# Decay rows spread by one transfer a head, rope tables by one transfer, and the last mLSTM head's statistics behind the first attention masks

## The chip, the cores and the metric

The kernel runs on one core of one Trainium2 chip. The metric is the device time of one execution in microseconds, as the median of several runs. TensorE (PE) multiplies, VectorE (DVE), ScalarE (ACT) and GpSimd (POOL) do the elementwise work, and transfers (DMA) are issued from the queues of SyncE (SP), ScalarE and GpSimd; all of them share the core's 16 DMA engines. Matrices go through TensorE as pairs of a rounded high part and a low part, three products for one.

## The reference

One block of a hybrid model, 512 tokens of width 1024, in float32. Half of the width is attention with 8 heads of 64, half is an mLSTM with 4 heads of 128.

```python
h = rms_norm(x, pre_norm_g)
proj = h @ w_in                      # 1024 -> 4*512 + 5*512 + 4 + 4
aq, ak, av, az, mq, mk, mv, mo, mz, mi, mf = split_columns(proj)

# attention: rotary positions on the first 16 of 64 dimensions of each head, causal softmax
ya = moba_attention(partial_rope(aq, pos), partial_rope(ak, pos), av)
ya = rms_norm(ya, attn_out_g) * silu(az)

# mLSTM: causal convolution over 4 tokens, gates mi, mf, decays between tokens
qk = silu(causal_depthwise_conv(concat([mq, mk]), conv_w, conv_b))
hm = mlstm_chunkwise(q, k * 128 ** -0.5, mv, mi + i_bias, mf + f_bias)
#   s = (q . k) * exp(D - m_t), D a causal matrix from sums of log-gates
#   h = num / max(|nq|, exp(-m_t))
hm = (hm - mean) * rsqrt(var + 1e-6) * mlstm_out_g
ym = sigmoid(mo) * hm * silu(mz)

y = concat([ya, ym]) @ w_out
out = x + rms_norm(y, post_norm_g)
```

## The kernel before, in words

The token axis is cut into 4 tiles of 128. The projection runs through 74 weight slots of 512 columns (SLOTS), the output through 16 more; a slot's weights come by one load of SyncE (L564) into one of 4 raw buffers, are rounded by ScalarE to a high part (L783, `cut`), and VectorE, or GpSimd for the last ones, takes the low part (L1070, L673, L677), after which the raw buffer is free for the load four slots on. All engines run programs written out by hand; each has a loop over the slot number b in which the work that goes beside that slot stands in a fixed order, with semaphores between engines. TensorE works slot b while ScalarE and VectorE cut slot b + 6. So each engine's queue is strictly in order: what waits holds what stands behind it.

The mLSTM is computed in its full 512 by 512 form, head by head. For head h and key tile j TensorE makes scores in bank 6 (`head_scores`), VectorE multiplies them by decays (`weighted`, L1198), ScalarE and VectorE split the result, and TensorE multiplies by the values (`head_values`). The next scores wait for `weighted`, since they use the same bank. The decays are exp(g[key] terms + g[query] terms): a row of 512 query terms for each of the 4 heads, kept in `rows[4]` (16 rows: 4 copies of 4 heads), must be spread over all 128 partitions. GpSimd makes the rows (L651) and writes them to memory (L653, `g_dram`). ScalarE's queue issues four transfers a head (`decay_rows`, L851), each of which reads one row, or its last 384, 256 or 128 elements, 128 times: the part of the row that key tile j needs. GpSimd adds the causal mask to the first 128 columns of each part (`decay_mask`, L659), waiting for all four, and ScalarE takes the exponential (`decays`, L841). All of this is for one head at a time in one buffer, so the rows of head h + 1 go out when the last tile of head h is weighted. For head 0 they go out at slot 16, and its exponentials stand at slots 20 and 21.

The rotary tables: ScalarE scales them by the norm of each token (L859), TensorE transposes them, ScalarE copies them out (L864), GpSimd writes them to memory (four times 16 KB, L683) and spreads them over the 8 heads by two transfers, one for cosines and one for sines (L687). VectorE uses them in `kq_rows` (L1263 and on).

`head_stats` (L1218 to L1239) takes mean and variance of two token tiles of an mLSTM head and `head_norm` (L1241 to L1249) normalises them; between the two stands a reciprocal root on GpSimd (`head_rsqrt`, L644). There are 8 of each. The last, number 7, is taken at the last slot (b = 64) by VectorE, and its norm at step 1 of the attention.

The attention is a second loop, over steps s, 32 units of a tile and a head (`unit`). In step s VectorE masks the scores (`mask`, L1383), ScalarE takes the exponential (L988), TensorE transposes, and the rest of the projection (the gates mz and mo), the turns and the output products are spread over the steps by a table (EVENTS). Around its start VectorE also takes the low parts of the queries (`q_low`, L1281), and gates (`mz_gate`, L1342); GpSimd multiplies the mLSTM rows by their gains (`ym_gain`, L712) and by the gate (`ym_gate`, L718), and VectorE finishes them (`z_gate`, L1350).

## Time and profile before

| | before |
|---|---|
| median of 3 runs | 320.37 us (319.39 to 320.59) |
| the profiled execution, its own time | 319.19 us |
| span of that execution, first to last instruction | 317.4 us |
| TensorE matmul busy | 307.7 us (97%) |
| VectorE busy | 223.6 us (70%) |
| ScalarE busy | 165.1 us (52%) |
| GpSimd busy | 88.1 us (28%) |
| granted TensorE clock, mean | 0.991 |
| moved by DMA | 38.30 MB, mean 121 GB/s |

Times of instructions count from the start of the span. Busy time of TensorE is the time in which a matmul is in flight, so a busy TensorE may still be fed below its best pace; consecutive starts show the pace. The granted clock is 1.0 at the full 2.4 GHz and 0.5 at 1.2 GHz. The chain that ended last is followed backwards from the end of the program, at each step to what released it. A wait for several semaphores is put down to the one that came last.

### The profile page before, as it was taken

The numbers are of one execution on the slowest core, as the hardware profiler recorded it, in microseconds if no ns is written. First come the engines' busy times: TensorE is split into PE (matmuls) and PEld (weight loads), VectorE is DVE, ScalarE is ACT, GpSimd is POOL, SyncE is SP. The second block draws the span as 40 slices with busy tenths as digits, with TensorE's granted clock in tenths as the row PEclk, the third lists the DMA queues.
The fourth block names the chain that finished last, engine by engine and source line by source line (L and its number), as shares of the span: only waits on it lengthen the run. The fifth ranks groups of instructions, "written<-read, shape, count | busy, mean of one in ns | idle before, by whom it ended". The sixth has DMA issues, their size and how long they took to land.

```text
span 317.4 us, 5020 instructions
## 1 busy us (share of the span) xinstructions
PE 307.7 (97%) x1607; PEld 258.1 (81%) x1607; DVE 223.6 (70%) x510; ACT 165.1 (52%) x339; POOL 88.1 (28%) x104
## 2 busy tenths in 40 slices
PE   8999999997999999999999999999999999999992
PEld 5788888876888888888888889978888888888882
DVE  2544899915999579976999547995577766856534
ACT  3467684548337421594243763485556976453201
POOL 4501003043541004000040006596711984000000
PEclk9999999997999999999999999999999999999998
DMA  7933463666452556753456423312220374310111
GB/s 219 322 77 91 127 191 86 140 158 183 112 111 68 160 101 177 230 166 93 124 172 208 134 74 94 102 33 69 66 66 2 126 187 153 135 66 1 68 66 66
DMA packets 30601, 38.30 MB, mean 121 GB/s; under 512 B 2664, under 2 KB 17872, under 8 KB 30576
## 3 DMA queue, kind: packets, MB, share of 16 engines
q1 hardware_dynamic: 27440, 34.51, 36.2%
q10 hardware_dynamic: 2464, 2.76, 5.0%
q0 software_dynamic: 672, 0.72, 0.8%
q8 instruction: 13, 0.21, 0.3%
q14 instruction: 12, 0.10, 0.1%
HBM read 33.68 MB, written 4.29 MB: 120 GB/s over the span
## 4 chain that ended last, share of the span: by engine, by line
PE 77%; DVE 11%; issue 5%; ACT 2%; DMA 2%; POOL 0%; DVEq 0%; POOLq 0%; ACTq 0%
PE bank L1512 20%; PE bank L1514 19%; PE bank L1513 19%; PE bank L1565 4%; PE bank L1869 3%; PE bank L1834 3%; PE bank L1813 3%; DMA w_raw<-in_w_in 2%; DVE w_lo L1070 2%; PE bank L1660 2%; DVE farena L1178 1%; PE bank L1763 1%; DVE rarena L1281 1%; PE bank L1545 1%; PE bank L1527 1%
## 5 line engine op out<-in xcount | busy, mean ns | idle before, releaser
L783 ACT ACTIVATE w_hi<-w_raw 128x512 fp32r<-128x512 f32 (+1 forms) x73 | 44.5, 616 | 71.2 <-PE bank L1514 47.2
L1512 PE MATMUL bank<-w_hi,xT_hi 128*128 128x512 f32 (+2 forms) x180 | 71.0, 395 | 0.4 <-DVE gy L1342 0.4
L1514 PE MATMUL bank<-w_hi,xT_lo 128*128 128x512 f32 (+2 forms) x180 | 68.0, 378 | 0.0
L1513 PE MATMUL bank<-w_lo,xT_hi 128*128 128x512 f32 (+2 forms) x180 | 67.7, 376 | 0.0
L1070 DVE TENSOR_TENSOR w_lo<-w_raw,w_hi 128x512 fp32r<-128x512 f32 (+1 forms) x66 | 45.7, 703 | 14.2 <-ACT w_hi L783 14.0
L1512 PE MATMUL bank<-xT_hi,w_hi 128*128 128x512 f32 x136 | 54.5, 401 | 0.0
L1514 PE MATMUL bank<-xT_hi,w_lo 128*128 128x512 f32 x136 | 53.5, 393 | 0.0
L1513 PE MATMUL bank<-xT_lo,w_hi 128*128 128x512 f32 x136 | 53.4, 393 | 0.0
L1514 PEld LDWEIGHTS bank<-w_hi,xT_lo 128*128 128x128 f32 x180 | 33.8, 188 | 5.8
L1512 PEld LDWEIGHTS bank<-w_hi,xT_hi 128*128 128x128 f32 x180 | 33.9, 188 | 5.5 <-issue 0.6
L1513 PEld LDWEIGHTS bank<-w_lo,xT_hi 128*128 128x128 f32 x180 | 34.0, 189 | 4.5
L1514 PEld LDWEIGHTS bank<-xT_hi,w_lo 128*128 128x128 f32 x136 | 25.8, 189 | 5.7
L1513 PEld LDWEIGHTS bank<-xT_lo,w_hi 128*128 128x128 f32 x136 | 25.9, 190 | 4.7
L1512 PEld LDWEIGHTS bank<-xT_hi,w_hi 128*128 128x128 f32 x136 | 25.8, 190 | 4.7
L644 POOL TENSOR_TENSOR vr<-vs,mhalf 128x2 f32<-128x2 f32 x8 | 5.6, 706 | 77.8 <-DVE vs L1237 77.8
L996 ACT ACTIVATE rarena<-bank 128x512 fp32r<-128x512 f32 (+3 forms) x32 | 14.0, 436 | 21.6 <-PE bank L1869 21.6
L1383 DVE CUSTOM_DVE_ANT_0 farena<-bank,causal 128x512 f32<-128x512 f32 (+3 forms) x32 | 15.3, 482 | 11.2 <-PE bank L1813 11.2
L1389 DVE TENSOR_TENSOR rarena<-bank,rarena 128x512 fp32r<-128x512 f32 (+3 forms) x32 | 15.6, 487 | 7.9 <-ACT rarena L996 7.8
L1198 DVE SCALAR_TENSOR_TENSOR farena<-bank,farena 128x512 f32<-128x512 f32 (+3 forms) x16 | 7.9, 491 | 17.1 <-PE bank L1514 17.0
L988 ACT ACTIVATE farena<-farena,mx 128x512 f32<-128x512 f32 (+3 forms) x32 | 17.9, 558 | 3.1 <-DVE mx L1383 2.9
L1178 DVE SCALAR_TENSOR_TENSOR farena<-farena,pcol 128x512 f32<-128x512 f32 x24 | 18.8, 783 | 0.9
L1869 PE MATMUL bank<-ident,farena 128*128 128x128 f32 x80 | 14.7, 281 | 0.0
(212 smaller groups left out, 563.8 us busy)
## 6 DMA issues: line engine op xcount, KB each, us to landing
w_raw<-in_w_in SPq DMA_DIRECT2D x66, 256.0 KB, 2.9
w_raw<-in_w_out SPq DMA_DIRECT2D x16, 256.0 KB, 2.6
kq_rows<-stage SPq DMA_DIRECT2D x8, 256.0 KB
gy<-kq_rows SPq DMA_DIRECT2D x8, 256.0 KB, 3.5
gy<-in_x SPq DMA_DIRECT2D x4, 512.0 KB, 5.3
out_y<-gy SPq DMA_DIRECT2D x7, 256.0 KB, 2.1
w_raw<-in_w_in SPq DMA_DIRECT2D x8, 196.0 KB, 3.5
farena<-in_x SPq DMA_DIRECT2D x4, 256.0 KB, 4.7
```

Source lines behind the costliest of these rows:

```text
L783: a.activation(hi, raw, ACT.Copy).then_inc(w_hi_done, 1)
L988: a.activation(prob[:, s % 2, 0:n], sm[:, s % 2, 0:n], ACT.Exp, scale=-1.0, bias=mx[:, s:s + 1], accum_out=rsum[:, s:s + 1]).then_inc(prob ...
L996: a.activation(pT[:, 2 * (u % 2), 0:n], bank[4 + u % 2][:, 0:n], ACT.Copy).then_inc(pt_hi, 1)
L1070: v.tensor_tensor(lo, raw, hi, ALU.subtract).then_inc(w_lo_done[n % 2], 1)
L1178: ins = v.scalar_tensor_tensor(out=acc, in0=u[:, j:j + SEQ], scalar=tap[j], in1=acc, op0=ALU.mult, op1=ALU.add)
L1383: v.tensor_tensor_reduce(sm[:, s % 2, 0:n], bank[6 + s % 2][:, at:at + n], causal[:, SEQ - n:], -Q_SCALE, BIG, ALU.add, ALU.min, mx[:, s:s ...
L1389: v.tensor_tensor(pT[:, 2 * (u % 2) + 1, 0:n], bank[4 + u % 2][:, 0:n], f32(pT[:, 2 * (u % 2), 0:n]), ALU.subtract).then_inc(pt_lo, 1)
L1512: pe.matmul(o, hi, m_hi, start=start, stop=False)
L1513: pe.matmul(o, hi, m_lo, start=False, stop=False)
L1514: return pe.matmul(o, lo, m_hi, start=False, stop=stop)
L1565: mm = pe.matmul(bank[t][:], xs[:, k, t * P:(t + 1) * P], ws, start=k + term == 0, stop=False)
L1869: mm = pe.transpose(bank[4 + u % 2][:, j * P:(j + 1) * P], prob[:, u % 2, j * P:(j + 1) * P], ident[:])
```

## The change

The decay parts become slices of one buffer of 1280 elements. GpSimd writes the rows of `g_dram` as 4 rows (one a head) of 1280 elements, in four transfers, one for each key tile, waits for them, and issues one transfer of 128 rows of 5 KB for a head; ScalarE issues none. For heads 1 to 3 that issue stands ahead of the reciprocal root of the head before. The rotary tables are scaled into another place in mixed order (cosine and sine of one dimension side by side), so that each row in memory holds both, and one transfer of 4 KB rows spreads them. The last head's statistics (`head_stats(7)`) go from slot 64 to step 1, behind the masks of steps 0 and 1 and the low parts of the queries; its reciprocal root on GpSimd goes to step 1; its norm goes to step 2, behind the gates; and GpSimd's four gain products go from steps 0 and 1 to steps 2 and 3.

```diff
--- before.py
+++ after.py
@@ -102,6 +102,7 @@
 R_MV, R_QK, R_P, R_KT, R_V, R_SIZE = 0, 4160, 6208, 8768, 12864, 16960
 R_PT, R_OUT, R_QT = 0, 2048, 4608
 P_AT = [0, 512, 896, 1152]
+P_END = 1280
 
 NU = NT * AH
 
@@ -313,7 +314,8 @@
                 else v.rearrange("p (a b c) -> p a b c", a=shape[0], b=shape[1])
 
         x_sb = f_part(F_X, NT, D)
-        decay = [f_part(F_E + P_AT[j], SEQ - P * j) for j in range(NT)]
+        decay_all = f_part(F_E, P_END)
+        decay = [decay_all[:, P_AT[j]:P_AT[j] + SEQ - P * j] for j in range(NT)]
         upad = f_part(F_U, 2, 516)
         cacc = f_part(F_ACC, 2, SEQ)
         pm = f_part(F_PM, 2, SEQ)
@@ -331,6 +333,7 @@
         by_dims, whole = stage, gate
         rope_t = [f_part(F_COS, SEQ), f_part(F_SIN, SEQ)]
         rope_flat = f_part(F_SIN, P)
+        rope_mixed = silu_az[:, 0, 0:P]
 
         def by_block_order(ap):
             return ap.rearrange("p (m h j) -> p h m j", m=4, h=AH)
@@ -374,8 +377,8 @@
             return blocks(w_hi[:, at]), blocks(w_lo[:, at])
 
         kq_dram = nc.dram_tensor("kq_rows", (2, AH, DH, SEQ), F32, kind="Internal").ap()
-        rope_dram = nc.dram_tensor("rope_rows", (2, ROT, SEQ), F32, kind="Internal").ap()
-        g_dram = nc.dram_tensor("g_rows", (16, SEQ), F32, kind="Internal").ap()
+        rope_dram = nc.dram_tensor("rope_rows", (ROT, 2 * SEQ), F32, kind="Internal").ap()
+        g_dram = nc.dram_tensor("g_rows", (MH, P_END), F32, kind="Internal").ap()
 
 
         x_in = [sem(f"x_in{c}") for c in range(len(X_CHUNKS))]
@@ -650,10 +653,19 @@
             g.wait_ge(gmax_done, 1)
             g.tensor_tensor(rows[4], rows[1], rows[2], ALU.subtract).then_inc(grows_done, 1)
             g.wait_ge(grows_done, 1)
-            g.dma_start(g_dram, rows[4]).then_inc(g_out, 16)
+            for j in range(NT):
+                g.dma_start(g_dram[:, P_AT[j]:P_AT[j] + SEQ - P * j], rows[4][MH * j:MH * (j + 1), j * P:])\
+                    .then_inc(g_out, 16)
+            g.wait_ge(g_out, 16 * NT)
+
+            def decay_rows(h):
+
+                if h:
+                    g.wait_ge(pm_done, NT * h)
+                g.dma_start(decay_all, g_dram[h:h + 1].to_broadcast([P, P_END])).then_inc(g_back, 16)
 
             def decay_mask(h):
-                g.wait_ge(g_back, 16 * NT * (h + 1))
+                g.wait_ge(g_back, 16 * (h + 1))
                 for j in range(NT):
                     v = decay[j][:, 0:P]
                     g.tensor_tensor(v, v, causalT[:], ALU.add).then_inc(g_masked, 1)
@@ -677,19 +689,21 @@
                     g.tensor_tensor(lo, blocks(w_raw[:, n % RAW, :]), hi.bitcast(F32),
                                     ALU.subtract).then_inc(w_lo_done[n % 2], 1)
 
+            decay_rows(0)
             decay_mask(0)
             g.wait_ge(rope_flat_done, 1)
             for t in range(NT):
-                g.dma_start(rope_dram.rearrange("q j s -> (q j) s")[:, t * P:(t + 1) * P],
+                g.dma_start(rope_dram.rearrange("j (q s) -> (j q) s", q=2)[:, t * P:(t + 1) * P],
                             rope_flat[t * 2 * ROT:(t + 1) * 2 * ROT, :]).then_inc(rope_out, 16)
             g.wait_ge(rope_out, 16 * NT)
-            for q in range(2):
-                g.dma_start(rope_t[q], rope_dram[q:q + 1].to_broadcast([AH, ROT, SEQ])).then_inc(rope_spread, 16)
+            g.dma_start(f_part(F_COS, 2 * SEQ), rope_dram.unsqueeze(0).to_broadcast([AH, ROT, 2 * SEQ]))\
+                .then_inc(rope_spread, 16)
             for t in range(NT):
                 g.wait_ge(az_done, t + 1)
                 g.wait_ge(gain_in, 16)
                 g.tensor_tensor(silu_az[:, t, :], silu_az[:, t, :], gains[:], ALU.mult).then_inc(az_gained, 1)
             for h in range(1, MH):
+                decay_rows(h)
                 head_rsqrt(2 * h - 2)
                 decay_mask(h)
                 head_rsqrt(2 * h - 1)
@@ -702,8 +716,6 @@
                 cut(b + AHEAD)
                 if b == S_MZ + 3:
                     head_rsqrt(2 * MH - 2)
-                if b == LAST_SLOT:
-                    head_rsqrt(2 * MH - 1)
 
             def ym_gain(t):
 
@@ -738,9 +750,11 @@
                     elif kind == "y_fin":
                         g.wait_ge(msy_done, i + 1)
                         rsqrt(ry[:, i:i + 1], msy[:, i:i + 1]).then_inc(ry_done, 1)
-                if s < 2:
-                    ym_gain(2 * s)
-                    ym_gain(2 * s + 1)
+                if s == 1:
+                    head_rsqrt(2 * MH - 1)
+                if 2 <= s < 4:
+                    ym_gain(2 * s - 4)
+                    ym_gain(2 * s - 3)
                 if 3 <= s < 3 + NT:
                     ym_gate(s - 3)
 
@@ -841,22 +855,14 @@
                 a.activation(decay[j], decay[j], ACT.Exp, bias=aT[:, j, 4 * j + h:4 * j + h + 1])\
                     .then_inc(decay_done, 1)
 
-            def decay_rows(h):
-
-                if h:
-                    a.wait_ge(pm_done, NT * h)
-                else:
-                    a.wait_ge(g_out, 16)
-                for j in range(NT):
-                    a.dma_start(decay[j], g_dram[4 * j + h:4 * j + h + 1, j * P:].to_broadcast([P, SEQ - j * P]))\
-                        .then_inc(g_back, 16)
-
             def rope_scale():
 
                 a.wait_ge(rope_in, 16)
                 a.wait_ge(rx_done, 1)
                 for t in range(NT):
-                    a.activation(rope_sb[:, t, :], rope_sb[:, t, :], ACT.Copy, scale=rx[:, t:t + 1]).then_inc(rope_scaled, 1)
+                    a.activation(rope_mixed[:, t * 2 * ROT:(t + 1) * 2 * ROT].rearrange("p (j q) -> p q j", q=2),
+                                 rope_sb[:, t, :].rearrange("p (q j) -> p q j", q=2), ACT.Copy,
+                                 scale=rx[:, t:t + 1]).then_inc(rope_scaled, 1)
 
             def rope_evac():
 
@@ -925,8 +931,6 @@
                     a.wait_ge(gmax_done, 1)
                     a.wait_ge(gate_clear, 1)
                     a.activation(gate_rows[32:48, :], rows[2], ACT.Copy, scale=-1.0).then_inc(gneg_done, 1)
-                if b == S_QK + 6:
-                    decay_rows(0)
                 if b == ST_AT[0]:
                     a.wait_ge(aT_done, 1)
                     a.activation(emt[:], bank[7][:].rearrange("p (t c) -> p t c", t=NT)[:, :, 32:32 + MH],
@@ -934,8 +938,6 @@
                 for h in range(MH):
                     if b - 2 in PE_ST and PE_ST[b - 2][0] == h:
                         pm_high(*PE_ST[b - 2])
-                        if PE_ST[b - 2][1] == NT - 1 and h < MH - 1:
-                            decay_rows(h + 1)
                     for c in range(2):
                         if b == S_Q[h] + 2 * c + 5:
                             conv_silu(2 * h + c)
@@ -1251,7 +1253,7 @@
             def kq_rows(w, m):
 
                 projected(v, ("ak", "aq")[w], m)
-                v.wait_ge(rope_spread, 32)
+                v.wait_ge(rope_spread, 16)
                 if w and m == 0:
                     v.wait_ge(kq_out[0], 16 * NT)
                 if m:
@@ -1320,7 +1322,7 @@
                             v_low(m)
                 if S_AQ + 6 <= b < S_AQ + 6 + NT:
                     k_low(b - S_AQ - 6)
-                if b - 2 in PE_PV and PE_PV[b - 2][1] % 2 == 1:
+                if b - 2 in PE_PV and PE_PV[b - 2][1] % 2 == 1 and b < LAST_SLOT - 1:
                     head_stats(2 * PE_PV[b - 2][0] + PE_PV[b - 2][1] // 2)
                 for h in range(MH):
                     for c in range(2):
@@ -1468,9 +1470,9 @@
                 if s < NU:
                     mask(s)
                 if s == 1:
-                    head_norm(2 * MH - 1)
                     q_low(2)
                     q_low(3)
+                    head_stats(2 * MH - 1)
                 if 0 <= s - LAG_FOLD < N_WIDE and s % 2 == 1:
                     y2_sum(s - LAG_FOLD)
                 for kind, what in events:
@@ -1486,6 +1488,8 @@
                 for kind, what in events:
                     if kind == "mz_late":
                         mz_gate(*what)
+                if s == 2:
+                    head_norm(2 * MH - 1)
                 for kind, what in events:
                     if kind == "ya_half":
                         ya_half(*what, 0)
@@ -1619,7 +1623,7 @@
 
                 pe.wait_ge(par_done, 2)
                 pe.wait_ge(rope_scaled, NT)
-                pe.transpose(bank[6][:, 0:P], rope_sb[:].rearrange("p t c -> p (t c)"), ident[:]).then_inc(rope_ps, 1)
+                pe.transpose(bank[6][:, 0:P], rope_mixed, ident[:]).then_inc(rope_ps, 1)
 
             def gate_cols():
```

## Rows read from the trace of the kernel before

**Rows 1.** Waits of TensorE in the whole span: engine, line, releaser, us, times, longest.

```profile
PE bank L1512 <- DVE farena L1198: 2.5, 1, 2.5
...
PE bank L1512 <- DVE gy L1342: 0.4, 1, 0.4
```

**Rows 2.** Busy time by stretch; then granted clock, DMA share, GB/s.

```profile
63.00:65.00 2.00, 2.00 (x10) 1.67 (x9) 0.85 (x2) 0.63 (x1) 0.00 (x0) 1.00 0.69 44
...
72.00:80.00 8.00, 6.55 (x25) 5.59 (x26) 4.91 (x9) 6.82 (x12) 3.25 (x4) 0.79 0.63 168
...
77.00:203.00 126.00, 126.00 (x624) 107.97 (x622) 101.03 (x241) 61.41 (x105) 27.52 (x30) 1.00 0.50 136
```

**Rows 3.** Chain that ended last, 61 to 73 us: start, us, what.

```profile
61.25 6.94 DMA w_raw<-in_w_in
...
70.25 1.22 ACT farena L841 x2
...
72.62 0.69 DVE farena L1198
```

**Rows 4.** Timeline of TensorE, 70 to 77 us: start, us, line, operands.

```profile
70.29 0.39 PE L1513 MATMUL bank<-w_lo,xT_hi 128*128 128x512 f32 x1
70.52 0.39 PE L1514 MATMUL bank<-w_hi,xT_lo 128*128 128x512 f32 x1
73.45 0.66 PE L1512 MATMUL bank<-rarena 128*128 128x384 f32 x1 [2.54 <-DVE farena L1198]
...
76.58 0.39 PE L1514 MATMUL bank<-xT_hi,w_lo 128*128 128x512 f32 x1
```

**Rows 5.** Timeline of GpSimd, 50 to 74 us.

```profile
52.92 0.56 POOL L653 DMA_DIRECT2D g_rows<-gy  x1 [0.29 <-POOL gy L651]
67.66 2.24 POOL L659 TENSOR_TENSOR farena<-farena,causalT 128x128 f32<-128x128 f32 x4 [14.19 <-DMA farena<-g_rows]
69.84 2.01 POOL L683 DMA_DIRECT2D rope_rows<-farena  x4
```

**Rows 6.** Timeline of ScalarE, the first issues of decay rows.

```profile
56.06 0.84 ACTq L851 DMA_DIRECT2D farena<-g_rows  x2
```

**Rows 7.** DMA issues of 52 to 74 us: size, us from issue to landing.

```profile
farena<-g_rows ACTq DMA_DIRECT2D x1, 256.0 KB, 4.1
...
g_rows<-gy POOLq DMA_DIRECT2D x1, 32.0 KB, 1.9
```

**Rows 8.** DMA issues of the whole span: size, median us to landing.

```profile
w_raw<-in_w_in SPq DMA_DIRECT2D x66, 256.0 KB, 2.9
...
farena<-rope_rows POOLq DMA_DIRECT2D x2, 256.0 KB, 5.4
stage<-in_post_norm_g SPq DMA_DIRECT2D x1, 512.0 KB, 5.4
```

**Rows 9.** Chain that ended last, 203 to 212 us.

```profile
207.26 0.68 DVE hsc L1245
...
207.97 0.60 DVE gy L1247 x2
...
209.77 0.61 DVE gy L1342
```

**Rows 10.** Timeline of GpSimd and of VectorE, 208 to 224 us.

```profile
208.65 3.52 POOL L712 TENSOR_TENSOR gy<-gy,gains 128x512 f32<-128x512 f32 x2 [0.73 <-DVE gy L1247]
...
220.57 0.68 DVE L1350 SCALAR_TENSOR_TENSOR gy<-stage,gy 128x512 f32<-128x512 f32 x1
...
223.77 0.69 DVE L1383 CUSTOM_DVE_ANT_0 farena<-bank,causal 128x512 f32<-128x512 f32 x1 [1.92 <-PE bank L1813]
```

**Rows 11.** Timeline of GpSimd and of ScalarE, head 1's masks and exponentials.

```profile
92.52 2.80 POOL L659 TENSOR_TENSOR farena<-farena,causalT 128x128 f32<-128x128 f32 x4
...
98.61 1.28 ACT L841 ACT_TABLE_LOAD   x1
```

**Rows 12.** One line: VectorE's first use of the rotary tables.

```profile
L1263 DVE TENSOR_TENSOR stage<-bank,farena x2: 683/684/684, 114.6 to 151.8; 128x512 f32<-128x512 f32 x2
```

## The prediction, made before the changed kernel was run

> **What bounds the kernel now.** I read the waits of TensorE first, then its busy time by stretch, then the chain that ended last, then the timeline around the one large hole, and last the transfers. TensorE never rests for long: from 77 to 203 us it is busy for 126.00 of 126.00 us at the full clock [rows 2], and the page has it at 97% of the span. So the time is TensorE's own work, which this change leaves alone, plus the holes in it. There are two. One matmul of L1512 waited 2.5 us for VectorE's L1198, another 0.4 us for L1342 [rows 1].
>
> The large hole is at 71 us. Matmuls of 512 columns start 0.23 us apart, the last at 70.52, the next at 73.45, and the one at 76.58 is the first that is back at the old pace [rows 4]. In between the clock falls to its lower level, 1.2 GHz: the mean grant of 72 to 80 us is 0.79 [rows 2]. From 70.52 to 76.58 nine matmuls start, none of over 512 columns. At 0.23 us each they need 2.07 us and took 6.06, so **the hole costs 6.06 - 2.07 = 4.0 us**, at least, since three of the nine have 384 columns.
>
> What ended last before 73.45 is in the chain [rows 3]: the weight load of slot 26, issued at 61.25, took 6.94 us to land (68.19). Behind it, in one ScalarE queue, stand the cut of that slot, a table load, the exponentials of the first decay masks (70.25) and the next cut; VectorE can then weight the first scores (L1198 at 72.62), and TensorE restarts. From the landing to the restart it is 73.45 - 68.19 = 5.26 us. TensorE would be free at 70.52 + 0.23 = 70.75, so **there is no hole if slot 26 lands by 65.5**, 2.7 us sooner, and if the first two masks are there when ScalarE asks.
>
> Why did that load take 6.94 us where the median is 2.9 [rows 8]? The decay rows of head 0 went out just before, as four transfers from ScalarE's queue from 56.06 on [rows 6]. VectorE's addend masks on GpSimd could start only at 67.66, when the last had landed [rows 5]. All 640 KB thus took 67.66 - 56.06 = 11.6 us. From 63 to 65 us the DMA engines are 0.69 busy and move 44 GB/s [rows 2]: short rows of one source that occupy the engines and carry little. The loads queued beside them wait.
>
> **The change, part by part.**
>
> *Decay rows, head 0.* Removed: four issues from ScalarE's queue and the four transfers. Added: three more writes to memory (four of 4 rows, not one of 16), a wait of GpSimd for them, and one transfer of 128 rows of 5 KB, issued from GpSimd. GpSimd issues its write at 52.92 now [rows 5]; four such issues cost 2.0 us (L683's four took 2.01, rows 5), and a write lands 1.9 us after its issue [rows 7]. So the last is issued at 54.4, lands at 56.4 to 56.9, and the rows go out at about 57.0, 0.9 us later than now. Nothing else is queued behind the wait on GpSimd before the masks and rope rows that come after it anyway.
>
> How long they take no row shows. From below: 256 KB of the same rows landed in 4.1 us [rows 7], so 61.1. From above: the same 640 KB in their present form, 11.6 us, so 68.6. The nearest row is the 512 KB spread of the post-norm gain in 4 KB rows, 5.4 us [rows 8]; with a quarter more bytes that is 6.8, or less, since part of 5.4 is fixed. GpSimd's own 256 KB spreads, 5.4 against 4.1 from ScalarE, say that its queue may add about 1. I take 6.5 to 7, landing at 64.
>
> *Slot 26* is issued at 61.25 still, since VectorE's cut of slot 22 before it doesn't move. Bounds of its landing: 61.25 + 2.9 = 64.1 and 68.19 as now. Two things help: slots 24 and 25, which stand before it in the queue, no longer share the engines with rows sent at 56.06, and the large rows end some 3 us sooner. I take 65, nearer to the median, because the two overlap only from 61.25 to 64. Then TensorE is not stopped: 65 + 5.3 = 70.3, before 70.75. The first two masks need 2 x 0.56 = 1.1 us after the rows [rows 5], so they are there at 65.1, and are asked for at 65 + 70.25 - 68.19 = 67.1. What is late next is TensorE itself. **Gain 4.0 us**; each microsecond of slot 26 after 65.5 gives one back, and then part of what the low clock took, which is 4.0 less the wait of 2.5, or 1.5 us.
>
> Here a page speaks against the step. The rows move from ScalarE's queue to GpSimd's, where the write at 52.92 was issued in 0.56 us and the four at 69.84, while VectorE stood waiting, in 0.50 each [rows 5]: hardly a difference. The Trainium skill, "SBUF — State Buffer", section "Summary: rules for kernel authors", says to issue from ACT or SP when a DMA is to hide under VectorE, since descriptor generation on GpSimd starves in VectorE's faster modes. Were every one of the five issues held for one VectorE instruction, the rows would leave later; the 0.56 us does not show it, and this is the rival "half way" below.
>
> *Decay rows, heads 1 to 3.* Now issued by GpSimd once the head before is weighted. For head 1 they queue behind GpSimd's four gain products, and I put them 1 to 2 us later against the rest. Masks of head 1 are made from 92.52 to 95.3, and ScalarE turns to them at 98.61 [rows 11]: 3.3 us of cover. Cost nothing; without the cover it would be the same 1 to 2 us. In heads 2 and 3 nothing stands ahead of them on GpSimd.
>
> *Rope tables.* The four products write in mixed order, the same size; one issue instead of two of 256 KB that land in 5.4 [rows 8]. First use on VectorE is at 114.6 [rows 12], over 30 us after the landing. Nothing.
>
> *The last head's statistics.* VectorE's chain ends at the gate at 209.77 + 0.61 = 210.38, for which TensorE waited [rows 1, 9]. Both masks now come first, and the normalising (0.68 + 0.60 = 1.3 us, rows 9) goes behind the gates, into the next step. The gate ends 1.3 us sooner, at about 209.1, and the wait of 0.4 is gone; ScalarE's exponentials and tanh ahead of the gate start sooner too, since the statistics no longer stand before the masks. Bounds: nothing, if VectorE's low parts are slowed by GpSimd's cuts beside them, and the 0.4, as more than the wait can't be had. I take **0.4**, since the chain shortens by three times that. Moved with it: GpSimd's gains of the mLSTM rows, from 208.65 [rows 10] to about 213.5, my estimate: a mask, two gates and a low part of 0.6 to 0.7 us each, and their waits, now stand ahead of the normalising. Behind it come four products and a gate product of at most 1.76 us (3.52 for two, rows 10), so VectorE's gate at 220.57 would find its operand by 222.3. VectorE idles 1.92 us right after [rows 10], which hides the wait.
>
> Sum: 4.0 + 0.4 = 4.4 us off the profiled execution's 319.19, which holds a span of 317.4 and 1.8 around it; that gives 314.8. The median of the runs is 1.2 above that execution, 320.37, so **316.0**.
>
> **Rivals.**
>
> *Half way* (15%). Slot 26 lands late because each 2 KB packet now takes turns with a 5 KB one, or because GpSimd's issues are held up. Take 67: the restart is at 72.3, 1.5 us of idle stay and up to 1.5 of the low clock, so 1.4 to 2.9 us are gained with the second part: 317.5 to 319.0. For it: rows and load overlap for 3 us. Against: few packets of each remain by then. The Trainium skill, "DMA: Bandwidth & Descriptors", section "Queues, rings and completion order", lets an engine switch queues only at packet boundaries, which would be the first of these.
>
> *The hole moves* (8%). Something else stops TensorE at once, for instance slot 27's cut, ScalarE's queue with table loads, or the low clock comes in another place: about 320, no change. Against it: no wait in 126 us behind the hole [rows 2]. That the rows still take as long as now belongs here too, yet even 68.6 for the landing has the masks there at 69.7, not 70.25.
>
> *Slower* (5%). GpSimd is now alone on the path write, wait, spread, mask. ScalarE's exponentials are at 70.25 and need two masks, 1.1 us after the landing, so from a landing after 69.1 every microsecond is one more of hole. That is 12.1 us after the issue at 57.0, beyond the 11.6 of today. If it took 15, the masks would come at 73.1, 2.8 late, and the time be 320.4 + 2.8 - 0.4 = 322.8.
>
> *More* (4%): three of the nine matmuls are narrower than 0.23 us, so the hole cost up to 0.2 more, and the pause around 210 may have cost more than its wait: 315.4 or less.
>
> **How the numbers follow.** The full gain has 68%, and its own range is 315.0 to 316.8, from the second part at nothing or whole, 0.2 more in the first, and the spread of the runs (319.39 to 320.59). To leave out no more than 2 in 10 the range goes up through the half way case: 315.0 to 318.8. About 0.5% (1.6 us, so 318.8) can be told from no change. Faster by more: 0.68 + 0.04 + most of the half way case = 0.83; within it 0.12; slower 0.05.
>
> **What would show it.** The waits of TensorE no longer have L1512 behind L1198, and 72 to 80 us has a grant of 1.00. GpSimd's masks start at 63 to 65 rather than 67.66. ScalarE's cut of slot 26 starts at 64 to 65.5. The large transfer lands in 6 to 7.5 us. The wait for L1342 at 210 is gone; GpSimd's gains start after VectorE's fourth gate. TensorE stays at 126 of 126 us afterwards. It is wrong if slot 26 still lands after 67, if another wait of over 1 us appears before 80, or if VectorE stands at the mLSTM gate for more than 2 us.

## The result and the profile after

| | before | changed |
|---|---|---|
| median, measured side by side | 319.62 us (317.45 to 320.59, 6 runs) | 314.26 us (314.06 to 316.75, 6 runs) |
| the profiled execution, its own time | 319.19 us | 314.27 us |
| span of that execution | 317.4 us | 312.5 us |
| TensorE matmul busy | 97% | 98% |
| VectorE, ScalarE, GpSimd busy | 70%, 52%, 28% | 73%, 53%, 29% |
| granted TensorE clock, mean | 0.991 | 0.995 |

The changed kernel takes 0.9848 of the time, with an interval of 0.9805 to 0.9891. It was forecast faster, at 316.0 and between 315.0 and 318.8; it lies 0.7 us below that range. Between the two profiled executions 319.19 - 314.27 = 4.92 us are gained where 4.4 were forecast.

First the busy time by stretch in the changed kernel, with the columns of [rows 2]: time in TensorE, its weight loads, VectorE, ScalarE and GpSimd, then clock, DMA share, GB/s. The last two stretches are around the gate and over most of the projection.

```profile
72.00:80.00 8.00, 8.00 (x39) 6.66 (x39) 6.66 (x8) 5.93 (x10) 5.45 (x4) 1.00 0.47 131
203.00:212.00 9.00, 9.00 (x52) 6.93 (x51) 7.34 (x22) 6.07 (x13) 6.00 (x6) 1.00 0.17 62
80.00:190.00 110.00, 110.00 (x536) 93.30 (x535) 89.22 (x218) 52.76 (x89) 18.57 (x26) 1.00 0.47 139
```

From 72 to 80 us, 39 matmuls start where 25 did, at a grant of 1.00, not 0.79. The hole is gone, none has come behind it, and the chain that ended last is now TensorE's own: 94% of it, where before it was 77%, with 11% of VectorE. The shares from the profile's page:

```profile
PE 94%; issue 3%; DVE 0%; DVEq 0%; ACT 0%; POOLq 0%; POOL 0%; ACTq 0%
```

The timeline of GpSimd in the changed kernel, against [rows 5, 10] (start, us, line, operands, count, idle time before it and what ended it):

```profile
52.77 2.12 POOL L657 DMA_DIRECT2D g_rows<-gy  x4 [0.29 <-POOL gy L654]
56.23 0.57 POOL L665 DMA_DIRECT2D farena<-g_rows  x1 [1.34 <-DMA g_rows<-gy]
62.23 2.67 POOL L671 TENSOR_TENSOR farena<-farena,causalT 128x128 f32<-128x128 f32 x4 [5.43 <-DMA farena<-g_rows]
...
209.31 5.05 POOL L724 TENSOR_TENSOR gy<-gy,gains 128x512 f32<-128x512 f32 x4 [1.46 <-DVE gy L1249]
```

And ScalarE's, where slot 26 is cut:

```profile
63.86 0.63 ACT L797 ACTIVATE w_hi<-w_raw 128x512 fp32r<-128x512 f32 x1 [0.90 <-DMA w_raw<-in_w_in]
```

The masks start at 62.23, not 67.66. The load of slot 26, issued at 61.1, landed 2.7 us later at 63.8, not at 68.19. That is 1.7 us before the 65.5 that the prediction set as its limit.

**A table of losses.** The changed kernel runs the same 1607 matmuls in the same order as before. I laid the starts of TensorE's instructions of each execution beside those of the changed kernel's first one and read off where the distance grows. This is the measure for all that follows, because it splits one execution by place. The entries are the us by which an execution falls behind the changed kernel's first one, good to about 0.03:

| profiled execution of | start-up, to 9 us | hole at 71 | gate at 210 | at the end |
|---|---|---|---|---|
| before, as in the rows | 0.15 | 4.17 | 0.54 | 4.88 |
| before, once more | 2.40 | 3.05 | 0.55 | 6.01 |
| decay rows alone | 1.12 | 0 | 0.55 | 1.68 |
| statistics alone | 0.66 | 4.19 | 0 | 4.88 |
| rope tables alone | 0.66 | 4.38 | 0.54 | 5.57 |
| the whole change, once more | 0.38 | 0 | 0 | 0.38 |
| 2.5 KB between the old rows | -0.05 | 0 | 0.54 | 0.48 |
| the same, with the statistics | 0.56 | 0 | 0 | 0.54 |

### The profile page after: what moved, and what is told of

The parts are those of the page before. It is cut to its first block, busy times and chain, and to the rows that moved or that the text cites. A ratio compares the mean times of both kernels' runs of the same rounds, so it can differ in the third digit from the quotient of the medians.

```text
span 312.5 us, 5011 instructions
## 1 busy us (share of the span) xinstructions
PE 306.0 (98%) x1607; PEld 257.4 (82%) x1607; DVE 226.8 (73%) x510; ACT 165.2 (53%) x339; POOL 91.1 (29%) x110
## 4 chain that ended last, share of the span: by engine, by line
PE 94%; issue 3%; DVE 0%; DVEq 0%; ACT 0%; POOLq 0%; POOL 0%; ACTq 0%
PE bank L1516 25%; PE bank L1518 24%; PE bank L1517 24%; PE bank L1569 4%; PE bank L1873 3%; PE bank L1817 3%; PE bank L1838 3%; PE bank L1664 2%; PE bank L1767 1%; PE bank L1531 1%; PE bank L1549 1%; PE bank L1828 1%; PE bank L1665 1%; PE bank L1850 0%; PE bank L1542 0%
## 5 line engine op out<-in xcount | busy, mean ns | idle before, releaser
L1072 DVE TENSOR_TENSOR w_lo<-w_raw,w_hi 128x512 fp32r<-128x512 f32 (+1 forms) x66 | 46.5, 715 | 9.7 <-ACT w_hi L797 9.5
```

What stands on the lines that cost most here:

```text
L1072: v.tensor_tensor(lo, raw, hi, ALU.subtract).then_inc(w_lo_done[n % 2], 1)
```

## Experiments

### The three parts, each alone

The first three runs are the change cut along its seams; the diffs are the parts of the diff above.

**Decay rows alone** (`g_dram`, `decay_all`, `decay_rows` of the diff):

> Only the decay rows: four writes and one transfer of 5 KB rows from GpSimd; rope tables and statistics as before. Theory A (the hole at 71 us is all that the rows cost): 4.2 us under the kernel before in a profile like the one on record, no wait of TensorE before 80 us, the wait of 0.4 us for the gate of L1342 still there near 206. Rival B (the gain is shared, the statistics or the rope tables carry a good part of it): 3 us or less.

Measured: 315.46 us (315.11 to 315.98), ratio 0.9888 [0.9858, 0.9917]. No wait for the weighting, and the gate's is still there. Its profiled execution, at 315.98, is only 3.2 us under before's and not 4.2; the table says why: the hole's 4.17 are gained, and 1.0 more was lost at the start.

**The last head's statistics alone** (`head_stats`, `head_norm`, `head_rsqrt`, `ym_gain` of the diff):

> Only the last head's statistics, root, norm and the gain products moved; rows and rope as before. Theory A: the hole at 71 us stays as long as before (2.5 us of wait and a low clock), the wait for the gate is gone, 0.4 to 0.7 us under before. Rival B: more than 1 us, as VectorE's chain ahead of the gate held TensorE in more ways than its wait shows. Rival C: nothing, as something else is late by the same amount.

Measured: 319.11 us (317.50 to 319.73), ratio 0.9994 [0.9973, 1.0015]. By its total this run tells nothing; by the table the gate's 0.55 us is gone and the hole has stayed at 4.19.

**Rope tables alone:**

> Only the rope tables in mixed rows and one transfer. All theories: within 0.3 us of before, as they are first used 35 us after they land. If the single transfer of 512 KB disturbs the weight loads beside it, slots 28 to 31 land later, which the margin of over 15 us between cut and use hides.

Measured: 319.90 us (318.04 to 320.91), ratio 1.0013 [0.9991, 1.0034]: nothing. The one 512 KB transfer lands 8.9 us after its issue, and nobody waits.

So the decay rows carry 4 of the gain, the statistics 0.55, the rope tables nothing.

### How much the kernels vary by themselves

**The kernel before, unchanged:**

> The kernel before once more, for a second profile. Theory A (its runs differ because the hole at 71 us differs): the hole in this profile is not the same 4.2 us but longer or shorter, and span minus hole minus 0.1 is the same 313.2 us within 0.3. Rival B (chips or runs differ everywhere): the hole is the same and the rest of the span differs.

Measured: 319.61 us (317.48 to 320.31), ratio 0.9993 [0.997, 1.0016]. Neither expectation held: the hole differed, and so did the rest of the span, at its start.

**The changed kernel, unchanged:**

> The changed kernel once more, for more runs and a second profile. Theory A (two holes are gone; what is left that differs between runs is the start, up to 2.3 us over the luckiest, as in the second profile of before): no wait of TensorE after 8 us, runs from 314.1 to 316.8, the second profile's difference from the first lies before 9 us. Rival B (the changed kernel is as steady as its first six runs said): all runs within 0.5 us of 314.3 but for a stray one.

Measured: 314.49 us (314.34 to 314.68), ratio 0.9844 [0.9812, 0.9876]. Rival B held.

Of the changed kernel's twelve runs eleven lie between 314.06 and 314.68 and one at 316.75; the kernel before varies by 3 us. Two rows of the second execution of before show how, TensorE alone, at the start and around the hole (us, busy us and matmuls, clock, DMA share, GB/s), and then the same stretch of the start in the changed kernel:

```profile
4.00:8.00 4.00, 3.81 (x12) 1.00 1.00 297
72.00:80.00 8.00, 5.21 (x26) 1.00 0.55 143
```

```profile
4.00:8.00 4.00, 4.00 (x20) 1.00 0.92 279
```

At the start the matmuls stand 0.43 us apart up to 9.1 us, and not 0.23: 12 in 4 us where 20 fit, for 2.4 us of loss. The 1.00 in the column of the granted clock doesn't contradict this, and is no measurement: this execution's record of the granted clock begins at 10.1 us only, and the column has 1.00 where there is no record. Matmuls of this size have this spacing where the record has the lower level, for instance behind the hole in the first profile of before, from 73.0 to 76.4 us:

```profile
74.55 0.63 PE L1512 MATMUL bank<-xT_hi,w_hi 128*128 128x512 f32 x1
74.98 0.63 PE L1513 MATMUL bank<-xT_lo,w_hi 128*128 128x512 f32 x1
```

So the slow start is most likely the lower level of the clock, lasting longer here than in other executions. Where the record begins earlier, the spacing changes earlier: with the rope tables alone it begins at 6.8 us and the spacing goes from 0.43 to 0.23 at 6.9; in the first profiles of before and of the changed kernel it begins at 4.8 and 5.4, and the spacing is 0.23 from 5.7 on. At the hole TensorE waited 2.8 us, longer than the 2.5 of [rows 1], and yet the clock stayed at its full level, so this hole cost 3.1 and not 4.2. The kernel before thus lost 0.15 or 2.4 us at the start and 4.2 or 3.1 at the hole, and the change removes only the second.

### Is it the queue, the number of transfers, or something else?

The prediction put the slow transfer down to "short rows of one source". These runs take the form apart, all without the statistics and the rope part. **One transfer of 5 KB rows, but from ScalarE's queue:**

```diff
+                a.dma_start(decay_all, g_dram[h:h + 1].to_broadcast([P, P_END])).then_inc(g_back, 16)
```

> Like rows_only, with the single 5 KB transfer of each head issued from ScalarE's queue, where the four stood. Theory A (the form of the rows matters, not the queue): the rows land by 62 to 63, slot 26 by 65, no hole, the time of rows_only within 0.5 us. Rival B (it is the queue): slot 26 lands after 66 and the hole is over 1 us.

Measured: 315.74 us (315.58 to 317.53), ratio 0.9896 [0.9852, 0.994]. It landed in 5.0 us, no hole. It isn't the queue.

**Four transfers, from GpSimd,** reading parts of the new 5 KB row:

> Like rows_only, with four transfers of the four parts a head (2, 1.5, 1 and 0.5 KB rows) from GpSimd's queue. Theory A (form, not queue): all four take 9 to 11 us as before, so they land at 66 to 68, slot 26 lands after 66 and a hole of 1.5 to 3 us comes back. Rival B (queue): no hole, within 0.5 us of rows_only.

Measured: 316.89 us (315.26 to 317.51), ratio 0.9906 [0.9877, 0.9935]. The four landed in 4.9, 4.6, 4.7 and 4.9 us, and the profiled execution, at 315.68, has no hole. The median is 1.4 above the decay rows alone all the same: four of the nine runs lie at 315.3 to 315.8 and five at 316.9 to 317.5, and none of those five was profiled, so what they lost is open. My theory for this run, that four short transfers are slow as such, fell here. Two things were still mixed: the queue, and the place in memory from which the parts are read.

**The changed kernel with three more transfers of 640 KB ahead of the first head's rows,** read from the same `g_dram` into unused memory:

```diff
+                if h == 0:
+                    for i in range(3):
+                        g.dma_start(r_part(R_KT + i * P_END, P_END).bitcast(F32),
+                                    g_dram[i:i + 1].to_broadcast([P, P_END])).then_inc(extra_in, 16)
...
             decay_rows(0)
+            g.wait_ge(extra_in, 48)
             decay_mask(0)
```

> The changed kernel with three more 5 KB transfers ahead of head 0's rows (1.9 MB into a place that is free then, not used). It measures the margin. Theory A (the rows themselves come late): slot 26 lands by 66, rows at 66 to 68, ScalarE's exponentials wait for the masks, hole of 0.5 to 2 us. Rival B (large packets hold the weight loads up, as in my half way case): slot 26 lands after 67, behind the rows, and ScalarE waits for it with the hole at 2 us or more.

Measured: 318.39 us (316.56 to 320.06), ratio 0.9965 [0.9931, 1.0]. The rows landed at 68.4, 10.3 us after their issue and after the three extra ones, so the added wait held nothing. Slot 26's load took 6.7 us, its cut had to wait until 68.22, and the hole was back at 4.03 us: rival B. This confirms the chain of the prediction in the other direction: keep the DMA engines occupied until 68 us, here by 1.9 MB that nobody needs, and slot 26 comes late and TensorE stops.

**Four transfers from ScalarE's queue, as before, but from the new rows:**

```diff
+                for j in range(NT):
+                    a.dma_start(decay[j], g_dram[h:h + 1, P_AT[j]:P_AT[j] + SEQ - P * j].to_broadcast([P, SEQ - P * j]))\
+                        .then_inc(g_back, 16)
```

> Rows of head 0 as four transfers issued by ScalarE, as before, but read from the new layout in memory (one row of 1280 elements per head, written by four transfers). Theory Q (ScalarE's queue with four parts is the slow pair, whatever the layout): the four land some 8 to 11 us after their issue, the masks start at 66.5 to 68.5 us, slot 26's load lands after 66, the hole at 71 is 1.5 to 3 us, and the time is 318 to 320. Rival L (the old layout, separate rows of 2 KB for each key tile, made them slow): the four land in 4.5 to 6 us, the masks start at 62 to 64, no wait of a score matmul for the weighting, 315.2 to 316.5.

**Four transfers from GpSimd, from the old 16 rows:**

> Rows of head 0 as four transfers from the old layout in memory (16 rows, one write), but issued by GpSimd. One write only, so the issue is at about 55.5 to 56 us. Theory Q (the queue decides between four slow and four quick parts): each lands in 4.5 to 6 us, masks start at 61.5 to 63.5, no hole, 315.2 to 317.5. Rival L (the layout decides): they land in 8 to 11 us, masks start at 66 to 68, the hole is there, 318 to 320.

Measured: 315.17 us (314.91 to 315.46), ratio 0.987 [0.9832, 0.9908], for the first; 316.09 us (315.48 to 317.74), ratio 0.9911 [0.9881, 0.9941], for the second. The transfers of the first and of the second, and those of before that [rows 7] leaves out (size, us from issue to landing):

```profile
farena<-g_rows ACTq DMA_DIRECT2D x1, 192.0 KB, 5.1
farena<-g_rows ACTq DMA_DIRECT2D x1, 128.0 KB, 5.1
farena<-g_rows ACTq DMA_DIRECT2D x1, 64.0 KB, 5.3
```

```profile
farena<-g_rows POOLq DMA_DIRECT2D x1, 192.0 KB, 5.0
farena<-g_rows POOLq DMA_DIRECT2D x1, 128.0 KB, 6.3
farena<-g_rows POOLq DMA_DIRECT2D x1, 64.0 KB, 8.7
```

```profile
farena<-g_rows ACTq DMA_DIRECT2D x1, 192.0 KB, 6.4
farena<-g_rows ACTq DMA_DIRECT2D x1, 128.0 KB, 8.2
farena<-g_rows ACTq DMA_DIRECT2D x1, 64.0 KB, 10.1
```

With the new rows the same four transfers from the same queue are quick, and with the old rows they are slow from either queue, if less so from GpSimd's, where a wait of 0.7 us for the weighting stays. The theory of the queue as the cause fell; what decides is the memory that is read. The queue still has a share: rival L had put the second run at 318 to 320. Why the old rows are less slow from GpSimd's queue, no run shows.

### The place of the rows

Key tile j of head h is read from row 4j + h, so the parts of one head lie four rows apart, which is 8 KB where rows are 2 KB. (Part j also begins 512 j bytes further inside its row. This is so in every run of this section, and the distances here are from row to row.) **The kernel before with 2.5 KB from row to row and nothing else:**

```diff
-        g_dram = nc.dram_tensor("g_rows", (16, SEQ), F32, kind="Internal").ap()
+        g_dram = nc.dram_tensor("g_rows", (16, SEQ + P), F32, kind="Internal").ap()[:, 0:SEQ]
```

> The kernel before with one thing changed: the 16 rows of decay terms lie 2.5 KB apart in memory and not 2 KB; one write, four transfers from ScalarE's queue, as before. Theory P (the place of the rows in memory makes the later parts slow: parts j of 1 to 3 read rows 8 KB further on each): with another pitch, 10 KB between the parts, the four land in about 4, 5, 5 and 5.5 us, the masks start at 62 to 64, slot 26's load lands before 65.5, no hole at 71, 315.5 to 317. Rival W (the place is of no matter; what counts is that the parts stand in separate rows, or that one transfer wrote them): the four land in 4, 6, 8 and 10 us as before, the masks start at 67 to 68.5, the hole stays, 318 to 320.

Measured: **314.93 us** (314.71 to 315.24), ratio 0.9881 [0.9836, 0.9926]. One number of one line gives all that the decay rows of the change gave. TensorE's start around 71 us and its one wait left, for the gate:

```profile
70.33 0.40 PE L1514 MATMUL bank<-w_hi,xT_lo 128*128 128x512 f32 x1
70.57 0.34 PE L1512 MATMUL bank<-rarena 128*128 128x384 f32 x1
```

```profile
PE bank L1512 <- DVE gy L1342: 0.4, 1, 0.4
```

Where [rows 4] has 2.93 us between two starts, there are 0.24 here.

**The old places, written by four transfers and not one:**

```diff
+            for j in range(NT):
+                g.dma_start(g_dram[MH * j:MH * (j + 1), :], rows[4][MH * j:MH * (j + 1), :]).then_inc(g_out, 16)
```

ScalarE waits for all four before it issues.

> The kernel before with one thing changed: the 16 rows are written by four transfers of 4 rows each and not by one of 16; the same places in memory, four spreads from ScalarE's queue. The last write lands at about 56.5 to 57, the spreads go out from there. Theory P (the place of the rows decides): still slow, the last part lands 9 to 10.5 us after its issue, masks at 67.5 to 69.5, the hole of 2.5 us or more stays, 318 to 320.5. Rival W (the single write decides, the four writes or the microsecond later that they bring heal it): the parts land in 4.5 to 5.5 us, masks at 63 to 64.5, no hole, 315 to 316.5.

Measured: 319.72 us (317.78 to 320.81), ratio 1.0011 [0.9981, 1.004]; the parts land in 4.4, 6.9, 8.0 and 9.9 us. How they were written is of no matter.

**4 KB from row to row** (`(16, 2 * SEQ)` in the same line), so 16 KB between parts:

> The kernel before with the 16 rows of decay terms 4 KB apart in memory and not 2 KB, nothing else. With 2.5 KB the parts of key tiles 1 to 3 took 65, 46 and 27 ns a packet, with 2 KB 166, 120 and 169 on average. Theory D (distances between the parts of a head that are multiples of 8 KB make them slow: 8 KB before, 16 KB here): the last part lands 8 to 11 us after its issue, the hole at 71 stays at 2 us or more, 318 to 320. Rival N (only near rows disturb each other, or any move of the rows heals it): 4.5 to 5.5 us for each part, no hole, 314.5 to 316.

**64 bytes more** (`(16, SEQ + 16)`):

> The kernel before with the 16 rows 2,112 bytes apart (64 more than before), so that the parts of a head lie 8,448 bytes apart and not 8,192 before the offset inside the row. Theory D (multiples of 8 KB are slow, everything else is not): each part lands in 4 to 5.5 us, no hole, 314.5 to 316. Rival G (the distance must differ by more than 256 bytes for the parts to fall into different places, as 2.5 KB rows do): parts as slow as before, 8 to 10 us for the last, hole of 2 to 3 us, 317.5 to 320.

Measured: 319.14 us (317.12 to 319.97), ratio 0.9992 [0.9963, 1.0021], for 4 KB; 315.51 us (314.99 to 317.56), ratio 0.9899 [0.9863, 0.9935], for 64 bytes more. For 4 KB theory D held; 64 bytes more came out between its two expectations, with a hole of 0.2 us left. What one packet of each part took in the DMA records, mean ns of 128, worked out from one execution of each (a packet is one row of one partition):

```
distance of the parts       2048 B  1536 B  1024 B  512 B   last part lands after
8 KB (before)                   92     166     120    169   10.1 us
16 KB (4 KB rows)              105     157     141    183    9.9 us
8 KB + 256 B (64 B more)        98      77     133     27    7.3 us
10 KB (2.5 KB rows)            113      65      46     27    5.1 us
```

A packet of 512 bytes needs 27 ns where nothing holds it up and took 169 on average, the longest 1014. The average differs from execution to execution: 68 to 241 in the other four profiles with 8 KB between the parts and ScalarE's queue; the last part landed after 9.9 to 10.3 us in all of them. The first part is about equally quick everywhere; the later ones are slow where the parts are 8 or 16 KB apart. 256 bytes beside that distance heal half of the landing time, with one of three parts still slow, and 2 KB all. The Trainium skill, "DMA: Bandwidth & Descriptors", section "Latency and other measured facts", has a row on the pitch of memory rows at large powers of two: at 4 MiB a copy runs at half its rate, a few KiB of padding restore it and 192 B do not; its cause, channels of the memory that many streams meet at once, is called there an inference. The trace agrees in kind, at distances far smaller than the page names. No run here shows what in the memory does it, so the cause below the distance stays open.

**2.5 KB rows and the statistics:**

> The kernel before with the rows 2.5 KB apart and with the last head's statistics moved, nothing else of the change. If the row's place gives the whole gain at 71 us and the statistics give 0.55 us, as the runs so far say, the time is 314.93 less 0.55, 314.4, within 0.3 of the changed kernel's 314.26 to 314.49; no wait of TensorE for the weighting and none for the gate. Rival: one transfer a head and the issue from GpSimd bring something of their own, and the changed kernel stays at least 0.5 us ahead: 314.9 or more here. The other side: ScalarE's issues, which GpSimd no longer makes, come earlier and give a further 0.3 to 0.5 us: 314.0 or less.

Measured: 314.78 us (314.31 to 316.44), ratio 0.9871 [0.9839, 0.9904]. This is between the two expectations. Its execution in the table differs from the changed kernel's only by 0.56 us of start-up. The changed kernel's two sets are 314.26 and 314.49, so if one transfer a head brings anything of its own it is 0.3 to 0.5 us, which these runs don't tell from the start-up. No kernel was found that beats the changed one.

## Why the prediction was right and where it was wrong

**What bounds the kernel: right.** The hole at 71 us was the only large loss, slot 26's load was behind it, and the engines busy with decay rows were behind that. With quick rows the hole was gone, and putting other traffic in their place brought it again. The rule for no hole, slot 26 landed by 65.5, held, with the limit at 65.3 rather. This is where slot 26 landed in each execution, its start-up taken off, and what was lost at the hole while the clock stayed at its full level:

| run | slot 26 landed | lost at the hole |
|---|---|---|
| changed, one from ScalarE's queue, 2.5 KB rows | 63.84, 63.90, 63.76 | 0 |
| 64 bytes more | 65.44 | 0.19 |
| GpSimd from the old rows | 66.25 | 0.97 |
| 4 KB rows | 67.85 | 2.56 |
| four writes | 68.11 | 2.83 |
| before, once more | 68.30 | 3.05 |

In the last five the loss is the time by which slot 26 landed after 65.27, within 0.03. The four executions in which the clock fell (before, statistics alone, rope tables alone, three more transfers) lost 1.4 to 1.6 us on top, where the prediction had 1.5. In no execution did the masks decide: with GpSimd from the old rows ScalarE's first cut in this stretch waited until 65.78 for slot 25's load, slot 26's cut stood behind it, and after a table load the exponentials followed at 68.51 without a wait.

**The hole's price: 4.0 forecast, 4.17 measured.** The rows' own working was low by the three narrower matmuls, as it had said. But it is one of two sizes: where the clock stays up, it is 2.6 to 3.1 (2.6 in the run with 4 KB rows, after a wait of 2.3 us).

**Time of the rows: near in its number, wrong in its reason.** Forecast 6.5 to 7 us from an issue at 57.0, landing at 64; measured 5.9 from 56.23, landing at 62.2. The reason, short rows of one source, is refuted: the same short rows land in 5 us from other places. What failed here is the reading of [rows 2]: 0.69 busy at 44 GB/s was taken as what short packets look like. A packet's own time stood in the same trace, 25 ns in the quickest and 169 on average for 512 bytes, and would have told that they were being held up. The upper bound of 11.6 us for "the same 640 KB" was a bound for old places only. For the step from four transfers to one, the right price was 0.

**Slot 26: mis-sized.** 65 forecast, 63.8 measured, with 2.7 us to land, under the median of 2.9. The rows were in at 62.2, so they shared the engines with it for 1 us and not 3. The rival of packets taking turns with 5 KB ones cost nothing that can be seen here; with three more such transfers, which shared the engines with it until the end, the same load took 6.7 us.

**The rule on issuing from GpSimd.** GpSimd's issues took 2.12 us for four and 0.57 for one beside a busy VectorE, and the masks came 5.0 us after ScalarE's single issue (56.80 to 61.83) and 6.0 after GpSimd's (56.23 to 62.23). The Trainium skill, "SBUF — State Buffer", section "Summary: rules for kernel authors", says that such issues starve in VectorE's faster modes. None was held up here, but no run shows whether VectorE was in such a mode, so this neither bears the rule out nor speaks against it. A difference of 1 us between the queues, as the prediction put it from [rows 8], is there.

**The gate: mis-sized.** 0.4 was taken from the wait's row; the matmul starts show 0.55. The wait of [rows 1] counts from the end of the matmul before, which is in flight for 0.27 us, while undisturbed the next starts 0.11 after its start: the 0.16 between them is lost too, and all 0.54 are lost at this one start. In the changed kernel the gates run with only a mask between them, then the norm:

```profile
204.82 1.28 DVE L1344 SCALAR_TENSOR_TENSOR gy<-gy,bank 128x512 f32<-128x512 f32 x2
...
206.64 1.28 DVE L1344 SCALAR_TENSOR_TENSOR gy<-gy,bank 128x512 f32<-128x512 f32 x2
...
208.62 0.60 DVE L1249 TENSOR_SCALAR gy<-num,mva,hsc 128x128 f32<-128x128 f32 x2
...
216.04 1.53 DVE L1352 SCALAR_TENSOR_TENSOR gy<-stage,gy 128x512 f32<-128x512 f32 x1
...
218.90 0.69 DVE L1385 CUSTOM_DVE_ANT_0 farena<-bank,causal 128x512 f32<-128x512 f32 x1 [0.72 <-PE bank L1817]
```

The gains start at 209.31, which with the 4.2 us of the hole is the 213.5 of the forecast. VectorE's gate at 216.04 takes 1.53 us beside GpSimd's last products where it took 0.68 [rows 10], and of the 1.92 us of idle time behind it 0.72 are left: hidden, as forecast, though with over half the cover gone.

**Heads 1 to 3 and the rope tables: nothing, right.** With the decay rows alone, TensorE's starts take no step of over 0.01 us against the changed kernel's between 9 and 204 us.

**From the profiled execution to the median: the term that failed.** On the footing of the profiled execution the forecast was 319.19 - 4.4 = 314.8, and 314.27 was measured; 0.17 of the hole, 0.15 of the gate and 0.15 of start-up, which had no term in the sum, make up the 0.5. Then 1.2 was added because the median of three runs lay that far above. That distance was carried over as if it belonged to every kernel. It didn't. Most of it, some 0.8, was the chance of three runs: larger sets of the same kernel have medians of 319.4 and 319.6. The rest, 0.2 to 0.4, is that runs of before differ in their hole and their start. The changed kernel's median and profiled execution are the same, 314.26 and 314.27. So the 1.2 should have been about 0. The range stood on the same term: with the 1.2 taken off it runs from 313.8 to 317.6, and the measured time lies inside.

## What to carry to other kernels

Where a transfer is slow for its size, compare the time of its packets with the shortest of the same size in the same trace; if they are held up, try the place of what it reads, by another distance between rows that are read at the same time, before its form or its queue: one number did what a rewrite did. Take a difference of two kernels on one footing, profile to profile, and don't carry a small sample's distance between profile and median through a change that removes what varies. Price a stall by the starts of the instructions after it against an undisturbed run, since the row of the wait counts from the end of the matmul before it and leaves out a clock that falls.

## What the hardware showed that I had not expected

- Parts of one small table read at once from places 8 or 16 KB apart: packets of 512 B take 68 to 241 ns on average in six executions, against 27 at 10 KB, and 64 KB land in 10 us, not 5.
- A wait of 2.3 to 2.8 us of TensorE left the granted clock at 1.00 in three executions (4 KB rows, four writes, before once more), and one of 2.4 to 2.6 us brought it to a mean of 0.79 over 8 us in four (before [rows 2], statistics alone, rope tables alone, three more transfers). The length of the wait doesn't decide it; what does is open.
- In three of the profiled executions (before once more, 4 KB rows, 64 bytes more) TensorE's first matmuls stand 0.43 us apart and not 0.23 up to about 9 us, for 2.4 to 2.6 us in all. The column of the granted clock has 1.00 there only because its record begins at 9.8 to 10.3 us; 0.43 is the spacing at the lower level elsewhere. Why that level lasts longer in these executions is open. The smaller losses at the start, up to 1.1 us, are open too.
